# Expert lookup of a PEER layer: chosen keys found with 16-bit integers and heads innermost

## The reference, cut to what matters

```python
q = (xb @ wq).reshape(T, 8, 2, 128)
s = einsum('thpc,hpkc->thpk', q, keys)            # 128 scores for each of two halves p
sv, si = top_k(s, 16)                             # values and indices, (T, 8, 2, 16)
cand = sv[:, :, 0, :, None] + sv[:, :, 1, None, :]         # 16 x 16 pairs
best, pos = top_k(cand.reshape(T, 8, 256), 16)
idx = take_along_axis(si[..., 0, :, None] * 128 + si[..., 1, None, :], pos)   # (T, 128) expert rows
gate = softmax(best)
act = gelu(einsum('ted,td->te', u_tab[idx], xb)) * gate
out = einsum('te,ted->td', act, v_tab[idx])
```

## Time and profile before

| what | us |
|---|---|
| median of 3 runs (lowest, highest) | 3221.85 (3213.39, 3231.14) |
| the profiled execution's own time | 3234.54 |
| its span, first to last instruction | 3232.6 |
| PE busy | 2891.0 (89%) |
| DVE busy | 1682.3 (52%) |
| POOL busy | 1555.5 (48%) |
| ACT busy | 557.7 (17%) |

### The profile page before, as it was taken

One profiled execution on the slowest core, in us unless ns is written; L12 is line 12 of the kernel. 1 busy time (PEld: TensorE's weight loads), 2 busy tenths in 40 slices (PEclk: granted clock), 3 DMA queues, 4 the chain that ended last, 5 costly groups with the idle time before them and its releaser, 6 DMA issues.

```text
span 3232.6 us, 29056 instructions
## 1 busy us (share of the span) xinstructions
PE 2891.0 (89%) x10143; PEld 1449.7 (45%) x10143; DVE 1682.3 (52%) x3842; ACT 557.7 (17%) x1190; POOL 1555.5 (48%) x1335
## 2 busy tenths in 40 slices
PE   5999989667789889956799999999999999999996
PEld 3656648433334445524244444444444444443331
DVE  4341124798998635897465654455654444441111
ACT  3211122100104555646000000000000000000000
POOL 2211213266675444546656665556665555553343
PEclk9999989888999999988899999999999999999998
DMA  3322254398899899998999999999999999998886
GB/s 133 120 100 74 85 197 146 116 363 287 308 355 364 310 365 361 376 339 340 402 378 381 396 365 386 390 382 399 372 378 394 373 379 382 372 393 289 284 296 230
DMA packets 338536, 998.63 MB, mean 309 GB/s; under 512 B 31095, under 2 KB 109687, under 8 KB 335832
## 3 DMA queue, kind: packets, MB, share of 16 engines
q0 software_dynamic: 184320, 671.17, 54.8%
q1 hardware_dynamic: 152344, 300.45, 26.1%
q10 hardware_dynamic: 1728, 25.17, 1.9%
HBM read 950.26 MB, written 46.40 MB: 308 GB/s over the span
## 4 chain that ended last, share of the span: by engine, by line
PE 60%; DMA 8%; DVE 7%; POOL 2%; issue 2%; ACT 1%; another core or an unknown queue 0%; SPq 0%; DVEq 0%; ACTq 0%; POOLq 0%
PE job_ps L1534 20%; PE wide_ps L1518 19%; PE v_ps L1555 9%; DMA v_rows<-in_peer_v,row_t 4%; PE job_ps L635 3%; PE wide_ps L635 2%; DVE u_row L1764 2%; POOL u_row L1444 2%; PE gate_ps L635 2%; DMA u_row<-in_peer_u,row_u 1%; PE wide_ps L1506 1%; DMA hand<-tmp_gates 1%; PE job_ps L613 1%; PE gate_ps L1506 1%; DVE prod L193 1%
## 5 line engine op out<-in xcount | busy, mean ns | idle before, releaser
L1454 POOL DMA_INDIRECT v_rows<-in_peer_v,row_t x640 | 693.7, 1084 | 785.7 <-PE v_ps L1555 617.2
L1444 POOL DMA_INDIRECT u_row<-in_peer_u,row_u x640 | 739.0, 1155 | 369.8 <-issue 178.3
L1764 DVE CUSTOM_DVE_ANT_0 u_row<-u_row,x_tile 128x1024 f32<-128x1024 f32 x640 | 771.0, 1218 | 115.3 <-DMA u_row<-in_peer_u,row_u 112.5
L1518 PE MATMUL wide_ps<-hand,arena 128*128 128x384 f32 x2048 | 688.0, 490 | 0.0
L1534 PE MATMUL job_ps<-arena 128*128 128x512 f32 x1536 | 687.1, 596 | 0.0
L1518 PEld LDWEIGHTS wide_ps<-hand,arena 128*128 128x128 f32 x2048 | 385.0, 190 | 322.0 <-issue 83.8
L1534 PEld LDWEIGHTS job_ps<-arena 128*128 128x128 f32 x1536 | 287.3, 190 | 368.9 <-issue 339.0
L1555 PE MATMUL v_ps<-v_rows,diag 128*32 128x512 f32 x2560 | 372.3, 621 | 66.1 <-DMA v_rows<-in_peer_v,row_t 65.3
L1802 DVE TENSOR_TENSOR arena<-arena,job_ps 128x512 f32<-128x512 f32 x192 | 131.6, 686 | 479.9 <-PE job_ps L1534 422.4
L899 POOL TENSOR_TENSOR exact<-arena,exact 128x1024 fp32r<-128x1024 f32 x48 | 118.0, 2463 | 451.6 <-ACT exact L647 451.6
L1656 ACT ACTIVATE hand<-wide_ps 128x384 f32<-128x384 f32 x128 | 62.9, 491 | 1494.8 <-PE wide_ps L1518 1196.6
(11 more groups left out here) (285 smaller groups left out, 2441.5 us busy)
## 6 DMA issues: line engine op xcount, KB each, us to landing
arena<-in_peer_ut SPq DMA_DIRECT2D x128, 512.0 KB
arena<-in_peer_v SPq DMA_DIRECT2D x128, 512.0 KB
hand<-tmp_gates SPq DMA_DIRECT2D x32, 768.0 KB
tmp_gates<-arena ACTq DMA_DIRECT2D x10, 2048.0 KB
arena<-in_w_in SPq DMA_DIRECT2D x32, 512.0 KB, 3.5
hand<-in_w_in SPq DMA_DIRECT2D x32, 512.0 KB
u_row<-in_peer_u,row_u POOLq DMA_INDIRECT x640
v_rows<-in_peer_v,row_t POOLq DMA_INDIRECT x640
```

The costliest lines, as they stand in the source:

```text
L1444: pool.indirect_dma_start(u_row[n % NU][:], None, dram["peer_u"], bass.IndirectOffsetOnAxis(row_u[g % 2][:, e:e + 1], 0)).then_inc(u_in[n ...
L1454: pool.indirect_dma_start(v_row[n % NV], None, dram["peer_v"], bass.IndirectOffsetOnAxis(row_t[g % 3][:, t:t + 1], 0)).then_inc(v_in[n % N ...
L1518: last = pe.matmul(wide[j % 2][:, 0:TD], uw[j % NW][:, k * P:(k + 1) * P], x_t[:, k], start=k == 0, stop=k == KD - 1)
L1764: dve.tensor_tensor_reduce(out=u_row[n % NU][:], in0=u_row[n % NU][:], in1=xb[g % 2][:], scale=1.0, scalar=0.0, op0=ALU.mult, op1=ALU.add, ...
```

## The change

`top_key` and `rank` become 16-bit unsigned integers with the heads innermost, [half][slot or choice][head], and a constant `slot` [slot][head] is made once from `iota`. `chosen_keys` runs once per tile, for all heads: 16 choices x 16 slots x 8 heads = 2048 elements of two bytes, in the same `prod` buffers. The sum over slots becomes four pairwise additions (8, 4, 2 and 1 slots wide), the last of which writes `key` in fp32. The number of steps (`yield`s) of a tile stays 8.

```diff
-        self.top_key = m.sb("top_key", [P, H, 2, TOPK])
+        self.top_key = m.sb("top_key", [P, 2, TOPK, H], U16)
         self.rank_u = m.sb("rank_u", [P, 2, H, TOPK], U32)
-        self.rank = m.sb("rank", [P, 2, H, TOPK])
+        self.rank = m.sb("rank", [P, 2, TOPK, H], U16)
+        self.slot = m.sb("slot", [P, TOPK, H], U16)
...
 def ranks(R, K, dve, s, lead):
-    s.did(dve.tensor_copy(R.top_key[:], K.top_at[:]))
...
+    for p in range(2):
+        s.did(dve.tensor_copy(R.top_key[:, p], K.top_at[:, :, p].rearrange("p h a -> p a h")))
     yield
     s.settle()
-    s.did(dve.tensor_copy(R.rank[:], R.rank_u[:]))
+    for p in range(2):
+        s.did(dve.tensor_copy(R.rank[:, p], R.rank_u[:, p].rearrange("p h r -> p r h")))
     yield
     s.settle()
...
+def chosen_keys(R, dve, s, work, key, ready=None):
+
+    pick = [w[:].bitcast(U16).rearrange("p (r a h) -> p r a h", r=TOPK, a=TOPK) for w in work]
+    full = [P, TOPK, TOPK, H]
+    for p in range(2):
+        s.did(dve.tensor_tensor(pick[p], R.rank[:, p].unsqueeze(2).broadcast_to(full),
+                                R.slot[:].unsqueeze(1).broadcast_to(full), ALU.is_equal))
+    yield
+    s.settle()
+    for p in range(2):
+        s.did(dve.tensor_tensor(pick[p], pick[p], R.top_key[:, p].unsqueeze(1).broadcast_to(full), ALU.mult))
+    yield
+    s.settle()
+    for n in (8, 4, 2):
+        for p in range(2):
+            s.did(dve.tensor_tensor(pick[p][:, :, 0:n], pick[p][:, :, 0:n], pick[p][:, :, n:2 * n], ALU.add))
+        yield
+        s.settle()
     if ready:
         dve.wait_ge(*ready)
     for p in range(2):
-        s.did(dve.tensor_reduce(key[:, p, half * n:half * n + n], pick[p].rearrange("p h r a -> p (h r) a"), X, ALU.add))
+        s.did(dve.tensor_tensor(key[:, p].rearrange("p (h r) -> p r h", h=H), pick[p][:, :, 0], pick[p][:, :, 1], ALU.add))
     yield
     s.settle()
...
-                for half in range(2):
-                    yield from chosen_keys(R, dve, r[0], prod, key, half, ready)
+                yield from chosen_keys(R, dve, r[0], prod, key, ready)
...
+            s.did(dve.tensor_copy(R.slot[:], R.iota[:, 0:TOPK].unsqueeze(2).broadcast_to([P, TOPK, H])))
+            s.settle()
             for _ in chosen(0):
                 pass
```

More of the change, by code:

```diff
@@ L107 @@
 TD = ND * P
+U16 = mybir.dt.uint16
 class Ranked:
@@ L180, in ranks @@
     s.did(dve.tensor_tensor(lead[:], K.best[:], K.best[:, :, 0:1].broadcast_to([P, H, TOPK]), ALU.subtract))
-    yield
-    s.settle()
-    s.did(dve.tensor_copy(R.rank[:], R.rank_u[:]))
[L184 to L191, removed]
     for p in range(2):
-        s.did(dve.tensor_tensor(pick[p].rearrange("p h r a -> p (h r) a"),
-                                R.rank[:, p, hs].rearrange("p h r -> p (h r)").unsqueeze(2).broadcast_to([P, n, TOPK]),
-                                R.iota[:, 0:TOPK].unsqueeze(1).broadcast_to([P, n, TOPK]), ALU.is_equal))
+        s.did(dve.tensor_copy(R.top_key[:, p], K.top_at[:, :, p].rearrange("p h a -> p a h")))
     yield
@@ L198, in chosen_keys @@
     for p in range(2):
-        s.did(dve.tensor_tensor(pick[p], pick[p],
-                                R.top_key[:, hs, p].unsqueeze(2).broadcast_to([P, 4, TOPK, TOPK]), ALU.mult))
+        s.did(dve.tensor_copy(R.rank[:, p], R.rank_u[:, p].rearrange("p h r -> p r h")))
     yield
     s.settle()
+def chosen_keys(R, dve, s, work, key, ready=None):
[15 more added lines that the diff above has]
+        s.settle()
     if ready:
```

## The result

| | before | after |
|---|---|---|
| median of 20 runs | 3222.16 | 3205.26 |
| lowest, highest | 3213.39, 3231.14 | 3193.35, 3213.13 |
| the profiled execution's own time | 3234.54 | 3198.09 |
| its span | 3232.6 | 3196.3 |

The ratio is 0.9941 with a 95% interval of 0.9932 to 0.9950: 16.9 us less by the medians, against 19 forecast and 3203 us predicted. Two later measurements of the same kernel, on other chips, gave 0.9926 (0.9906 to 0.9946) and 0.9926 (0.9907 to 0.9944); there the medians differ by 20.3 and 21.9 us. The two profiled executions shown first lie 36.4 us apart: that of before, 3234.54, was longer than any of its twenty timed runs, and that of after was the second quickest of its twenty.

A forecast was written before the change was run, and what follows sets the result against it. PE bounds most of the kernel and DVE the dips, where four lookups count: 5.2 + 5.6 + 5.6 + 4.7 = 21.1 us, less 2 for DMA, 19 us, so the median goes from 3221.85 to 3203 (3188 to 3224).

The forecast's parts named there:

- What bounds the kernel: PE mostly; DVE only in the dips, so four lookups of eight count, those of tiles 0, 1, 4 and 5.
- The new pairs: DVE's 16-bit lookup instructions go by bytes: 1.22 us for 2048 elements, 8.16 us a tile against 14.34.
- rival C: No packing in DVE's pairs: 16-bit runs one element a cycle like 32-bit; 2.2 us more, 3224; chance 0.12.
- Scattered access: Strided last addition and casts on DVE: 0.10 us more each, so 0.39 and 0.32 us.
- A tile: One tile's lookup and casts on DVE: 14.34 - 8.16 - 0.54 = 5.6 us saved (5.4 to 6.0).
- Tile 1, tile 4: Lookups of tiles 1 and 4: 5.6 us each, out of PE's waits of 13.8 and 21.9 us.
- Tile 5: Tile 5's lookup: ACT is next and idles for DVE only 1.48 and 3.21 us, so 4.7 us.
- The 2 us off for DMA: At 1410 to 1460 us DMA has 4.4 us of room for 10.3 wanted; 2 lost, between 0 and 5.9.
- The sum: Four tiles make 21.1 us, less DMA's loss 19 us: profiled execution 3215.5, median 3203.
- B: Lookups shrink but half reaches the end, a fetched row or ACT's turn being late next; 10 us saved, 3212; chance 0.22.
- D: Short 16-bit runs with repeats stall DVE in the first two pairs; 49.6 us on the path, 3271; chance 0.03.
- The signs to look for: Profile after: 1.2 us x16, PE's 6.5 us wait nearly gone, 21.9 near 16, DVE busy down some 40 us.

The follow-up runs named there:

- only_0145: New lookup in tiles 0, 1, 4 and 5 alone, the old one in the others; ratio to the kernel before 0.9933 (0.9916 to 0.9950).
- only_2367: New lookup in tiles 2, 3, 6 and 7 alone, the old one in the others; ratio to the kernel before 1.0002 (0.9990 to 1.0014).
- heads_outer: The changed kernel's 16-bit numbers with heads outermost and slots innermost; ratios to the kernel before 0.9941 and, measured again, 0.9938.
- before_again: The kernel before, unedited, profiled a second time; the profiled execution took 3227.67 us, its span 3225.7.
- only_01: New lookup in tiles 0 and 1 alone, the old one in the others; ratio to the kernel before 0.9969 (0.9955 to 0.9982).
- only_45: New lookup in tiles 4 and 5 alone, the old one in the others; ratio to the kernel before 0.9955 (0.9939 to 0.9971).
- after_again: The changed kernel, unedited, measured and profiled again on another chip; ratio to the kernel before 0.9926, span 3216.7 us.
- after_third: The changed kernel, unedited, measured and profiled once more on a third chip; ratio to the kernel before 0.9926, span 3217.4 us.

## Why the prediction was right

**What bounds the kernel.** Right, and the step that carried the forecast. The chain named four lookups of eight, and leaving the others old lost nothing that can be measured (only_0145: 0.9933), nor did they gain anything alone (only_2367: 1.0002).

**The new pairs.** The two ends were 1.22 and 2.28 us, and 1.22 was taken by the bytes argument. Measured 1.220, then 0.689, 0.426 and 0.287 for the additions (0.69, 0.42, 0.29 forecast). The choice was right for this layout and the reason too wide, as heads_outer shows: the upper end, 2.286, is reached with the same bytes. What rival C feared was a matter of the innermost step, not of the operation; and with the heads outermost it came for the compare alone, the product kept 1.218.

**Scattered access.** The last addition was put at 0.39 and took 0.369. The difference of 256 and 128 elements (585 and 369 ns) makes 1.69 ns an element for writes 16 words apart. The casts were put at 0.32 and took 0.262 to 0.266, against 0.39 at the upper end. The sum had kept the 0.10 us of the earlier trace rows for a stride. Writes cost 0.08 (0.369 less 0.29) and reads in a cast about 0.045 (0.264 less 0.218, the median of the dense casts in heads_outer).
The Trainium skill's figure for a step of 24 words (Vector Engine (DVE) Microarchitecture Reference, 5.2: 2.50 ns a column) would have made 0.19 by estimate. The 16-word step here is cheaper, 1.69 ns, and bears out the price of the earlier trace rows.

**A tile.** Forecast 5.6 us saved, measured 14.34 - 8.06 - 0.42 = 5.9, the casts' two steps having gone from 0.53 to 0.95 us. `slot` was put at 0.4; it takes 0.61, but the first DVE instruction of the part was slow before as well (0.64 us for L177), so that tile 0's stage is 5.7 shorter, not 5.2.

**Tile 1, tile 4.** 5.6 each forecast, 5.8 and 5.8 in the stages. For tile 1 the size was right and the wait incomplete. The prediction named the 13.8 us for the products behind the lookup. It overlooked the 5.1 us for tile 1's own row numbers, and these went, while the 13.8 became 15.3. That DVE has no gap in this stage, as the prediction says (52.58 busy of 53.1 us before, 46.71 of 47.6 after) is what made the sum come out whichever wait was named.

**The wait `ready`.** The prediction has it five steps later in the tile. By the code it stood before the fifth of eight steps and now stands before the eighth, three later. DVE waits for it in neither listing, so nothing hung on this.

**Tile 5.** This term was mis-sized: 4.7 forecast, 5.7 measured. ACT's idle time for DVE had been taken as 1.48 + 3.21 us. A third gap, ahead of the second eviction of that block, went as well, 5.5 together:

```profile
1459.05 0.60 ACT L1643 ACTIVATE arena<-wide_ps 128x512 f32<-128x512 f32 x1 [0.77 <-PE wide_ps L1506]
```

The 5.7 us are DVE's stage. ACT's own stretch from squares to squares went from 14.78 and 14.21 us (before, before_again) to 9.11, 9.09 and 9.31 in the three profiles of the change, 5.3 on average.

**The 2 us off for DMA.** The size came out about right and the place wrong; as 2 had been chosen between 0 and 5.9, the size is partly luck. The step said that from tile 0 to 700 us DMA's work "moves as a whole", and took the loss at 1410 to 1460 us. But R0-Z is 74.2 to 76.0 us in the four profiles with the old tile 0 and 77.1 to 79.5 in five of the six that have S-R0 at 10.8 (the first profile of after had 72.9): on average 74.8 and 77.4, 2.6 us given back where DMA is busy 0.96 to 1.00 of the time. Within a chip the step is 4 us (74.6 and 76.0 against 79.2; 74.2 against 77.1 to 79.5), but in the first pair of profiles it went the other way (74.4, 72.9), so its size is uncertain. At 1410 to 1460 us nothing was lost: L4-T4, T4-L5 and L5-R5 are 11.6 us shorter together, where 10.3 had been wanted, and behind them R5-E is 93.1 on average over the profiles of after and 93.2 over those of before. That the loss comes from DMA is argued from its share; no run changed the fetches.

**The sum.** By the averages of three profiles after and two before, the stages make -5.7 + 1.7 - 5.8 + 0.9 + 1.2 - 5.8 - 0.2 - 5.7 - 0.2 + 1.2 = -18.4 us, beside 19 forecast, 16.9 by the medians of twenty runs, and 24 by the two later ratios of 0.9926. The four stages of the lookup alone are 23.0 us shorter, where the prediction had 21.1 before its 2 us off; the terms of I-Q, Q-L4 and E-J are smaller than what these stages vary by in one kernel. The medians of three measurements fell by 16.9, 20.3 and 21.9 us, so that the first lies within about 2 us of the forecast is in part luck.

**The rivals.** B (half) is out with only_01 and only_45. C has its row in heads_outer, in another layout. D fell with 1.220 us. What B named as the next limit is there, though: with tile 1's lookup out of the way, 5 of 9 us came out and fetched rows stood in the chain.

**The signs to look for.** L199 at 1.2 us x16, the additions near 0.7, 0.4 and 0.3, PE's wait of 6.5 us down to 0.9, tile 5's exponential without a wait: all there. PE's wait of 21.9 us became 18.5, not 16: it is counted from where PE last finished something, and that varies with the execution (24.4 in before_again; 17.9 and 18.2 in after_again and after_third); the stage around it is 5.8 shorter. DVE's busy time fell from 1682.3 to 1636.3, 46 us, for 40 forecast.

## What to carry to other kernels

Cost a change to a shared routine call by call: four of eight calls stood on the chain, and they alone were worth anything. To get a two-input VectorE instruction to take 16-bit elements at twice the pace of fp32 ones, arrange the data so that a repeated operand repeats a run of neighbours (8, 16 and 128 here), not a single element; the layout made 1.22 against 2.29 us here for the same numbers. And before explaining a difference between two profiled executions, measure the same stages in a second profile of each kernel: here 20 of 36 us were not in the medians of twenty runs, while the stages that the change touches repeated to within about half a microsecond.

## What the runs showed that I had not expected

The product in heads_outer, which also repeats an operand, kept the full rate at 1218 ns; only the repeat of a single element halves it. Runs of two 16-bit neighbours with gaps between them cost as well: 386 ns for 256 elements, against 287 in long runs; in runs of four it was not so (423 ns for 512 elements in heads_outer, 426 in the change). A write of fp32 from 16-bit inputs, 16 words apart, costs 1.69 ns an element, and a dense write fed by single 16-bit reads 16 elements apart costs no less (heads_outer: 389 ns for 128 elements, 369 for the scattered write). And a gap of 10 us in one stage between profiles of one program (Q-L4, 486.5 to 496.6 us, on different chips) stands beside stages of DVE work that repeat to within half a microsecond; what sets it is open.
